# Which engine counts the narrowest block in a 31-step threshold search: from ScalarE to VectorE

## The reference

```python
dots = jnp.einsum('bthd,bsd->bths', qi, ki_all)
score = jnp.einsum('bth,bths->bts', wi, jax.nn.relu(dots))
score = jnp.where(allowed[None], score, -jnp.inf)
top_val, top_idx = lax.top_k(score, topk)      # topk = 256
logits = ...  # attention over the chosen 256 keys only
```

## Time and profile before

| what | us |
|---|---|
| median of 3 runs | 3011.31 |
| the three runs | 3008.76, 3011.31, 3017.05 |
| profiled execution, its own time | 3008.23 |
| its span, first to last instruction | 3006.5 |
| TensorE busy | 2856.5 (95%) |
| VectorE busy | 1643.6 (55%) |
| ScalarE busy | 987.3 (33%) |
| GpSimd busy | 648.8 (22%) |

### The profile page before, as it was taken

How to read it: one execution, slowest core, us unless ns; L and a number is a source line. 1 busy time by engine, 2 the same in 40 slices (tenths; PEclk the granted TensorE clock), 3 DMA queues, 4 the chain that set the end, 5 groups by cost and what they waited for, 6 DMA issues and landing times.

```text
span 3006.5 us, 43059 instructions
## 1 busy us (share of the span) xinstructions
PE 2856.5 (95%) x16186; PEld 2453.2 (82%) x16186; DVE 1643.6 (55%) x2804; ACT 987.3 (33%) x1260; POOL 648.8 (22%) x280
## 2 busy tenths in 40 slices
PE   5999889999999999999989989899999999999997
PEld 2778733379999999999977876234999999999996
DVE  7758777785452534524544777763435344344355
ACT  4246646533221111111233565563332111121112
POOL 2411410011222222222242034000112212222221
PEclk9999999999999999999999999999999999999999
DMA  5412100242222222212241311002112222222222
GB/s 218 138 64 85 37 22 1 57 162 84 84 84 70 84 70 84 86 54 85 76 135 47 123 43 37 1 1 64 43 64 91 64 76 80 73 84 72 82 83 86
DMA packets 71352, 224.95 MB, mean 75 GB/s; under 512 B 17232, under 2 KB 17488, under 8 KB 70096
## 3 DMA queue, kind: packets, MB, share of 16 engines
q1 hardware_dynamic: 70192, 219.36, 21.7%
q10 hardware_dynamic: 1056, 4.19, 0.3%
HBM read 211.44 MB, written 11.54 MB: 74 GB/s over the span
## 4 chain that ended last, share of the span: by engine, by line
PE 42%; issue 32%; DVE 11%; ACT 7%; POOL 4%; DVEq 2%; DMA 1%; ACTq 0%; POOLq 0%; SPq 0%
PE ps L980 33%; ACT notsel L779 5%; POOL w_lo L617 4%; PE ps L1238 2%; DVE smax L1732 1%; PE ps L1222 1%; PE ps L1031 1%; DVE hf L1389 1%; DMA w_ada<-in_w_ada 1%; PE ps L1226 1%; PE ps L1206 1%; DVE s_cand L1519 1%; DVE s_keep L1531 1%; PE ps L1228 1%; PE ps L1094 1%
## 5 line engine op out<-in xcount | busy, mean ns | idle before, releaser
L617 POOL TENSOR_TENSOR w_lo<-w_raw,w_hi 128x1024 fp32r<-128x1024 f32 x202 | 500.4, 2477 | 1852.8 <-ACT w_hi L730 1852.8
L980 PE MATMUL ps<-u_hi,w_hi 128*128 128x352 f32 (+1 forms) x2112 | 457.5, 325 | 2.1 <-ACT rstd L931 2.1
L980 PE MATMUL ps<-u_hi,w_lo 128*128 128x352 f32 (+1 forms) x2112 | 458.4, 325 | 0.0
L980 PE MATMUL ps<-u_lo,w_hi 128*128 128x352 f32 (+1 forms) x2112 | 455.6, 324 | 0.0
L730 ACT CAST w_hi<-w_raw 128x1024 fp32r<-128x1024 f32 x202 | 211.0, 1045 | 528.4 <-PE ps L980 337.7
L980 PEld LDWEIGHTS ps<-u_hi,w_hi 128*128 128x128 f32 x2112 | 362.1, 189 | 3.7 <-ACT rstd L931 2.7
L980 PEld LDWEIGHTS ps<-u_lo,w_hi 128*128 128x128 f32 x2112 | 361.0, 189 | 0.0
L980 PEld LDWEIGHTS ps<-u_hi,w_lo 128*128 128x128 f32 x2112 | 360.9, 189 | 0.0
L779 ACT ACTIVATE notsel<-score,s_cand 128x384 bf16<-128x384 f32 (+3 forms) x248 | 297.5, 1200 | 139.3 <-DVE s_cand L1519 139.1
L1830 DVE SCALAR_TENSOR_TENSOR x<-ps,mod,x 128x704 f32 (+2 forms) x240 | 125.5, 579 | 347.5 <-PE ps L980 341.1
L980 PE MATMUL ps<-a_hi,w_hi 128*128 128x352 f32 x1056 | 228.7, 325 | 4.3 <-POOL w_lo L617 2.1
(11 more groups left out here) (265 smaller groups left out, 4152.5 us busy)
## 6 DMA issues: line engine op xcount, KB each, us to landing
w_ada<-in_w_ada SPq DMA_DIRECT2D x96, 512.0 KB, 4.8
w_raw<-in_w_up SPq DMA_DIRECT2D x88, 512.0 KB, 3.4
w_raw<-in_w_in SPq DMA_DIRECT2D x34, 512.0 KB, 3.5
cw<-in_convw SPq DMA_DIRECT2D x32, 512.0 KB, 5.1
ada_later<-in_w_ada SPq DMA_DIRECT2D x24, 512.0 KB, 3.6
w_raw<-in_w_down SPq DMA_DIRECT2D x32, 384.0 KB, 3.1
w_raw<-in_w_down SPq DMA_DIRECT2D x32, 320.0 KB, 2.9
w_raw<-in_w_out SPq DMA_DIRECT2D x16, 512.0 KB, 3.5
```

Source lines behind the costliest of these rows:

```text
L617: nc.gpsimd.tensor_tensor(w_lo[slot][:], w_raw[:], w_hi[slot][:].bitcast(F32), ALU.subtract)\
L980: last = nc.tensor.matmul(ps[:, bank + t, 0:w], wt[slot][:, kk, :], mv[:, kk, t * TW:t * TW + w], start=(at == 0 and p == 0), stop=(at == ...
```

## The change

One tuple changes. Block 0 (384 scores) leaves `ON_ACT`.

```diff
-ON_ACT = (0, 4, 5, 6)
+ON_ACT = (4, 5, 6)
```

## The result

| | before | after |
|---|---|---|
| median us (6 runs each, on one chip) | 3010.03 (3003.07 to 3017.05) | 3031.65 (3029.57 to 3033.26) |
| ratio, 95% interval | | 1.0070 [1.0053, 1.0087] |
| span of the profiled execution | 3006.5 | 3029.5 |

What follows compares the result with a forecast made beforehand. Work between VectorE and ScalarE in the search was taken as almost even, with VectorE becoming last. Layer shifts of 1.46 and 1.76, less 0.4 for the recount, gave +2.8 us: 3014.1 against a 3011.31 median, range 3007 to 3021.

Steps and rivals of the forecast that it cites:

- The price of the count and of a round: Prompt search: VectorE's added 384-wide count costs 0.54 us, making an ordinary round 0.36 us longer.
- The gap of 0.09 before `s_keep`: VectorE in each round: with nothing to wait for, `s_keep` starts 0.09 us after the preceding instruction ends.
- Rounds 3, 7 and 11: a hold swallows the loss: VectorE held until GpSimd's `w_lo` ends takes ScalarE's earlier shift: -0.82, -0.72 and -0.26 us.
- Round 15: a new hold: `s_cand` comes 0.25 us behind `w_lo` and is held until 270.70; `s_keep` shifts +1.44 us (layer 1: +1.74).
- Rounds 16 to 26: "+1.08", and then only shifts: Rounds 16 to 18 add 1.08 us, making the last convolution group 2.52 late (layer 1: 2.82); later rounds carry shifts.
- "ScalarE gives 0.62 back" at 327 and 340 us: TensorE's waits follow ScalarE, which leaves 0.62 us earlier: lateness falls to 1.92 at 327.62; only 0.46 is available at 340.87.
- The wait at 340.87: TensorE's last listed wait in layer 0's search, forecast to end 1.46 us later (layer 1: 1.76).
- The range: Whole kernel, 8 in 10: 3007 to 3021 us; the forecast's own range was 3010 to 3018.5, from count and clock.
- "nothing is absorbed": Slower rival: each search round's shift reaches TensorE, 6.3 us a layer, 12.5 in all, or 3023.8; chance 10%.
- the second rival: No collision in round 15: `s_cand` still starts before `w_lo`, giving -1.0 us, or 3010.3; chance 22%.

Runs made afterwards that it cites:

- a_single: Changed kernel with `s_keep` (as `tensor_scalar`) and the predicated copy split into six one-column instructions each in rounds 18, 24 and 26: 3017.8 us, ratio 1.0033.
- a_pause3: Changed kernel with three small ScalarE copies before each `w_hi` cast at the end of rounds 18, 24 and 26: 3015.6 us, ratio 1.0025.
- b_dup: Kernel before, with VectorE also counting block 0 into an unread column while ScalarE keeps its count: 3024.8 us, ratio 1.0056.
- a_pause_15: Changed kernel with three small ScalarE copies before the casts behind rounds 14, 18, 24 and 26: 3012.8 us, ratio 1.0017.
- b_pause3: Kernel before, with three small ScalarE copies before the `w_hi` casts at the end of rounds 18, 24 and 26: 3012.5 us, ratio 1.0015.
- b_gate: Kernel before, with GpSimd waiting for `cand_ready` of rounds 7, 11 and 15 before starting `w_lo` there: 3001.4 us, ratio 0.9968.

## Why the prediction was wrong

Step by step, as the prediction put it:

- **The price of the count and of a round.** Nearly right: the count 0.54 as forecast, the round +0.41 in place of +0.36. The gap of 0.09 before `s_keep` came from a place that has no loop and no drain in front of it; in the rounds it is 0.15 to 0.17. In a_single, whose round 24 has the drain but stands outside the loop, it is 0.07 (327.68 to 327.75, before an `s_keep` of one column), so the loop rather than the drain seems to go with the longer gap.
- **Rounds 3, 7 and 11: a hold swallows the loss.** Right for 7 and 11. In round 3 there is hardly a hold (`s_keep` takes 0.32 in place of 0.17); my -0.82 let it start at the end of `w_lo`, where the earlier trace rows would have it end there. Counted from the first `s_cand` (200.82 after, 201.01 before), round 3's `s_keep` ends 0.89 earlier than before (forecast 0.82), round 7's `s_cand` 0.68 (0.72) and round 11's 0.08 (0.26).
- **Round 15: a new hold.** Right. The end of `s_cand` was forecast at 270.70 and is at 270.88 (271.07 if both traces start their search together), in both layers behind a hold of about 1.9 (`s_cand` takes 2.15 and 2.13). It is worth 3.2 us of search in the two layers.
- **Rounds 16 to 26: "+1.08", and then only shifts.** This is the step that failed. I walked on with the price of a round and looked for GpSimd only at the starts of runs, where the earlier trace rows had shown me `s_cand` held. I had even worked out that VectorE and ScalarE's followers move against each other by 0.98, for round 15. The same 0.98 had to be held against every pair in which a short VectorE instruction starts just ahead of a GpSimd one. At the end of rounds 18, 24 and 26 the margin was 0.98 or 0.99: my own numbers gave a dead heat, three times in each layer, with 2.2 us to lose each time and a fourth behind round 24. My sum had nothing for them. The runs show 2.33, 2.34, 2.25 and 2.33 us in place of 0.17 in layer 0 and the same in layer 1; taking these holds away with a_pause3 returns 14.7 us of search and +21 becomes +8.
- **"ScalarE gives 0.62 back" at 327 and 340 us.** The runs fit the mechanism: b_dup, in which ScalarE gives nothing back, costs +17, and a_pause_15, in which it does and no new hold is left, +5. But in the kernel after, the very earliness of ScalarE brings `w_lo` forward onto `s_keep`, and that takes more than it gives. The wait at 340.87, which I let end 1.46 later, ended 7.58 later.
- **The rest.** TensorE's clock adds to it: after the wait of 2.22 the four matmuls at 348.45 take 2.40 in place of 1.98, and from there to the end of layer 0's search 37.40 us pass in place of 35.53. Of these 1.87 us, 1.53 are the clock: TensorE runs 86 matmuls without a pause until VectorE's `cy` at 367.03, in 18.58 us at a granted clock of 0.91, where before it took 17.05 (340.87 to 357.92) at 1.00. Layer 1 has 18.71 in place of 17.04. The other 0.34 lie behind, with a new hold of 1.21 at 368.17. In a_pause3 the stretch takes 17.04 again (343.51 to 360.55), so this slower clock goes with the holds and is part of the 14.7.
- **The range.** It was made from the price of the count and the clock, with holds only at round 15. A dead heat should have made the range wide on the slow side. My rival "nothing is absorbed", 3023.8, was nearer in time, but for a wrong reason: three of the stalls that absorb were there.

Without any new hold my walk gave -1.0 (the second rival), and a_pause_15, which has none, costs +5 [+2, +8]. The copies may be part of that, as b_pause3 costs as much; how the rest splits into the 0.05 of each round and other things stays open.

## What to carry to other kernels

When an edit shifts two engines against each other, take the size of that relative shift and hold it against every margin between a short VectorE instruction and a GpSimd one near it, at the ends of runs as well as at their starts; any margin close to it is a cliff, and the range has to hold both sides. Short instructions that must not be held can be ordered by one more wait on a semaphore that some instruction already raises (b_gate). And a count of stalls is no sum of gains: removing one hold often brings the next pair together.

## What was unexpected

- A shift of 0.07 us (`w_lo` 0.03 ahead of a short instruction or 0.04 behind it) is worth 2.2 us, and it falls the same way in both layers. But the `s_cand` of round 29 that started 0.030 to 0.036 ahead of `q` was held, in nine cases of nine.
- The predicated copy of six columns is held like `s_keep` and `s_cand` (2.20 to 2.27 in place of 0.17), while one-column forms of all three run beside GpSimd, six of them in 0.82 us or less. For `s_cand` and the copy only the width differs in the program (the trace names the one-column copy COPY_PREDICATED_SCALAR); `s_keep` also became a `tensor_scalar`, so there the width isn't shown to be the reason.
- Two holds can follow one another: in round 24 `s_keep` waits for `w_lo`, and by then GpSimd's next instruction is in front of the copy.
